# The end of a two-layer DiT kernel: gate row multiplied on GpSimd, one joining pass on VectorE, last rows stored in halves

## What is computed

```
def rms_norm(x, gain):
    xf = x.astype(jnp.float32)
    y = xf * lax.rsqrt(jnp.mean(xf * xf, axis=-1, keepdims=True) + NORM_EPS)
    return (y * gain.astype(jnp.float32)).astype(x.dtype)
...
        x = x + gt_f * rms_norm(expert_choice_ffn(h, w_router[l], w_gate[l], w_up[l], w_down[l]), g_post_f)
...
    return x
```

## Time and profile before

| | |
|---|---|
| median of 3 runs | 1984.68 us |
| the profiled execution's own time | 1987.76 us |
| its span | 1986.0 us |
| TensorE busy | 1852.5 us (93%) |
| VectorE busy | 518.4 us (26%) |
| ScalarE busy | 457.9 us (23%) |
| GpSimd busy | 158.0 us (8%) |

### The profile page before, as it was taken

One profiled execution on the slowest core, in us unless ns is written; L12 is line 12 of the kernel. 1 busy time (PEld: TensorE's weight loads), 2 busy tenths in 40 slices (PEclk: granted clock), 3 DMA queues, 4 the chain that ended last, 5 costly groups with the idle time before them and its releaser, 6 DMA issues.

```text
span 1986.0 us, 28060 instructions
## 1 busy us (share of the span) xinstructions
PE 1852.5 (93%) x12106; PEld 878.1 (44%) x12106; DVE 518.4 (26%) x1178; ACT 457.9 (23%) x961; POOL 158.0 (8%) x225
## 2 busy tenths in 40 slices
PE   4999999999899999999999999989987998888886
PEld 2555555864333333333333555568642332233322
DVE  2020576742410000000002403467433110011113
ACT  4132123533311101110112404135331111111012
POOL 0000011110011111111111000021010000000000
PEclk8999999999899999999999999999998999999998
DMA  9311187012599999999999412130159999999996
GB/s 405 132 43 54 36 355 297 23 65 85 217 357 396 414 404 410 399 418 400 411 410 374 167 43 85 43 149 23 44 192 381 426 426 426 427 427 426 427 427 249
DMA packets 54028, 540.82 MB, mean 272 GB/s; under 512 B 6528, under 2 KB 8704, under 8 KB 22960
## 3 DMA queue, kind: packets, MB, share of 16 engines
q1 hardware_dynamic: 36704, 488.82, 59.2%
q0 software_dynamic: 17088, 50.67, 7.8%
q10 hardware_dynamic: 144, 0.01, 0.0%
HBM read 515.75 MB, written 23.72 MB: 272 GB/s over the span
## 4 chain that ended last, share of the span: by engine, by line
PE 81%; DMA 12%; DVE 5%; ACT 2%; issue 1%; SPq 0%; DVEq 0%; ACTq 0%
PE ps L2089 17%; PE ps L1691 10%; PE ps L2172 9%; PE ps L1924 7%; PE ps L1668 6%; PE ps L2097 6%; DMA ring<-in_wstream 5%; DMA work<-in_wstream 3%; DMA big<-in_wstream 3%; PE ps L1871 3%; PE ps L2179 3%; PE ps L2042 2%; PE ps L1844 1%; PE ps L1615 1%; PE ps L1660 1%; PE ps L1837 1%
## 5 line engine op out<-in xcount | busy, mean ns | idle before, releaser
L2089 PE MATMUL ps<-ring,work 128*32 128x512 f32 (+1 forms) x2560 | 342.6, 596 | 12.8 <-DMA ring<-in_wstream 10.2
L1528 DVE TENSOR_TENSOR work<-glao,ps 128x512 f32<-128x512 f32 x31 | 21.3, 687 | 772.8 <-ACT glao L940 399.5
L2089 PEld LDWEIGHTS ps<-ring,work 128*32 128x32 f32 (+1 forms) x2560 | 104.6, 116 | 242.7 <-issue 228.6
L1691 PE MATMUL ps<-hT,ring 128*128 128x512 f32 (+1 forms) x592 | 208.6, 511 | 3.5 <-issue 2.1
L2172 PE MATMUL ps<-big,work 128*32 128x512 f32 (+1 forms) x1216 | 163.5, 598 | 2.1 <-ACT work L900 2.1
L1691 PEld LDWEIGHTS ps<-hT,ring 128*128 128x128 f32 x592 | 112.9, 192 | 97.1 <-issue 87.1
L1924 PE MATMUL ps<-ring,hT 128*128 128x512 f32 x320 | 138.8, 592 | 0.0
L2097 PE MATMUL ps<-ring,work 128*32 128x512 f32 x1024 | 118.9, 594 | 0.0
L1668 PE MATMUL ps<-ring,hT 128*128 128x384 f32 (+3 forms) x384 | 110.9, 451 | 0.0
L2089 PE MATMUL ps<-big,work 128*64 128x512 f32 x384 | 86.6, 595 | 15.0 <-DMA big<-in_wstream 15.0
L1924 PEld LDWEIGHTS ps<-ring,hT 128*128 128x128 f32 x320 | 60.4, 191 | 72.2 <-issue 72.2
(11 more groups left out here) (330 smaller groups left out, 2177.3 us busy)
## 6 DMA issues: line engine op xcount, KB each, us to landing
ring<-in_wstream SPq DMA_DIRECT2D x150, 2048.0 KB, 16.8
big<-in_wstream SPq DMA_DIRECT2D x68, 2048.0 KB, 18.7
hT<-in_wstream SPq DMA_DIRECT2D x12, 1024.0 KB, 30.8
work<-in_wstream SPq DMA_DIRECT2D x12, 1024.0 KB, 33.4
x_kept<-big POOLq DMA_DIRECT2D x14, 512.0 KB, 3.5
big<-x_kept POOLq DMA_DIRECT2D x12, 512.0 KB, 5.5
work<-in_nat_bias POOLq DMA_DIRECT2D x32, 128.0 KB, 2.4
xn_lat<-big POOLq DMA_DIRECT2D x8, 512.0 KB, 3.8
```

Of the source, the lines that this page charges most:

```text
L1528: V.tensor_tensor(HIDL, SGL, bank(1), ALU.mult).then_inc(sem("hid"), 1)
L1691: last = T.matmul(bank(n % 4, tn), uw[:, j * D + kc * P:j * D + kc * P + P], hTv[:, kc, t0:t0 + tn], start=kc == 0, stop=kc == KC - 1)
L2089: last = T.matmul(bank(m)[r:r + block, :], XST[:, kc, e, b:b + block], gate_up[j][kk][:, m * D + h * 512:m * D + (h + 1) * 512], start=kc ...
```

## The change

In the second layer, GpSimd now multiplies `ACC` by the gate row (without the reciprocal) into one of two buffers `GAINED`, behind its loads of `X`. It waits for the tile's `acc`, and for the third and fourth tile also until the join of the tile two back has read the buffer. VectorE no longer scales: it takes the reciprocal, waits for `gained`, and computes `GAINED * rs + X` in one pass. It no longer waits for that pass's completion. The last tile is joined in two halves of 512 columns, each followed by its own store on SyncE.

```
+        GAINED = [GAIN_X, w(tokens_at + KC * 3 * CW, D)]
...
             for t in range(NLT):
                 sp.wait_ge(sem("x_ready"), t + 1 + (DEPTH - 1) * NLT)
-                sp.dma_start(out[t * P:(t + 1) * P, :], X[:, t, :]).then_inc(sem("stored"), 16)
-            sp.wait_ge(sem("stored"), 16 * NLT)
+                if t + 1 < NLT:
+                    sp.dma_start(out[t * P:(t + 1) * P, :], X[:, t, :]).then_inc(sem("stored"), 16)
+                else:
+                    for h in range(2):
+                        c = slice(h * D // 2, (h + 1) * D // 2)
+                        sp.wait_ge(sem("x_ready"), t + 1 + h + (DEPTH - 1) * NLT)
+                        sp.dma_start(out[t * P:(t + 1) * P, c], X[:, t, c]).then_inc(sem("stored"), 16)
+            sp.wait_ge(sem("stored"), 16 * (NLT + 1))
...
                     x_again()
+                    for i, t in enumerate(tiles(l)):
+                        if i >= 2:
+                            pool.wait_ge(sem("x_ready"), i - 1 + l * NLT)
+                        pool.wait_ge(sem("acc"), LAST_ACC + i + 1)
+                        pool.tensor_tensor(GAINED[i % 2], ACC[:, t, :], GROW_F[0], ALU.mult).then_inc(sem("gained"), 1)
...
                     link(V.reciprocal(rs[:, t:t + 1], ss[:, t:t + 1]))
-                    link(V.scalar_tensor_tensor(GAIN_X, ACC[:, t, :], rs[:, t:t + 1], GROW_F[0], ALU.mult, ALU.mult))
                     dve.wait_ge(sem(f"x_rows{t}"), X_AGAIN[l])
-                    V.tensor_tensor(X[:, t, :], X[:, t, :], GAIN_X, ALU.add).then_inc(sem("x_ready"), 1)
-                    dve.wait_ge(sem("x_ready"), t + 1 + l * NLT)
+                    dve.wait_ge(sem("gained"), i + 1)
+                    for a in range(0, D, D if i + 1 < len(ts) else D // 2):
+                        c = slice(a, a + (D if i + 1 < len(ts) else D // 2))
+                        V.scalar_tensor_tensor(X[:, t, c], GAINED[i % 2][:, c], rs[:, t:t + 1], X[:, t, c], ALU.mult, ALU.add).then_inc(sem("x_ready"), 1)
                     if i + 2 < len(ts):
                         last_add(i + 2)
```

More of the change, by code:

```diff
@@ L245, in bass_hybrid_dit @@
         SQUARES, GAIN_X = w(tokens_at, D), w(tokens_at + D, D)
+        GAINED = [GAIN_X, w(tokens_at + KC * 3 * CW, D)]
+        assert KC * 3 * CW >= 2 * D and tokens_at + KC * 3 * CW + D <= outputs_at
         GROW_F = [w(picked_at + D, D), w(picked_at, D)]
```

## The result

The changed kernel takes 1989.01 us (median of 12 runs, 1986.78 to 1990.0), the one before 1984.94 us (12 runs). The ratio is 1.0018, 95% interval 1.0010 to 1.0026: slower by some 3.6 us (2.0 to 5.2). The forecast was 1986.6 us in a range up to 1988.2.

The account below looks back on a forecast made before the run. VectorE's own work and the last store were taken to set the end. With joins held, VectorE ends 2.5 us later, half stores save 0.65: +1.9 us, 1986.6 us, range 1980.2 to 1988.2.

Parts of the forecast that it names:

- Held joins: At the program's end, GpSimd's multiplications hold VectorE's joins, which have two SBUF inputs: +1.9 us, 1986.6 us; chance 0.58.
- the order: Where third multiplication and second join become ready 0.02 us apart, GpSimd gets the port first; chance 0.34.
- the nearest row to the join: L1228, without PSUM operands, took 2.29 and 2.90 us beside GpSimd multiplications instead of 0.17; so joins are held.
- The rival in which additions are held: VectorE's last additions are held by GpSimd too, so nothing overlaps from 1968.1 on: 1988.0 us; chance 0.08.
- free overlap: VectorE's joins and GpSimd's multiplications run side by side without holding: 1980.4 us, bounds 1979.5 to 1981.6; chance 0.22.
- slow sharing: Joins and GpSimd multiplications share and both take longer, without outright holding: around 1983.5 us; chance 0.12.
- The size of the hold: VectorE's work at the program's end finishes 2.5 us later than 1982.9, with held joins at 1.28 us.
- the nearest row was exact: Each GpSimd multiplication of 128x1024 with both inputs full takes 2.35 us, bounds 1.89 and 2.75.
- The rival with VectorE first: The second join wins the port before the third multiplication: +0.7 us, 1985.4 us; chance 0.24.
- The half stores: Storing the last tile in halves ends the span 0.65 us earlier, bounds 0 and 0.7.
- GpSimd's drain: Not in the prediction, which had nothing queued behind GpSimd's multiplications and the span ending with the last store.

Follow-up runs that it names:

- the best version with GpSimd: Changed kernel with joins reading X from PSUM (copied by ScalarE) and the last tile's gate multiplication on VectorE: 1982.14 us, ratio 0.9982 to the kernel before.

## Why the prediction was wrong

**Held joins: right, with luck in the order.** The joins are held at every place that the forecast named. At the first, the second multiplication was already running. At the other two I had GpSimd ready 0.02 us ahead and gave it the port for that. In the records VectorE starts first, by 0.03 and 0.04 us, and the multiplications still keep their 2.35 us while the join is held; the same happens once where the last tile's multiplication is VectorE's (1973.75 and 1973.79). So the order was forecast rightly, but not for a reason that the records bear out: that part was luck. No run has the join clearly ahead of a multiplication, so what happens then is not shown.

The experiment with X in PSUM and the one with memsets show together that, for the joining pass, the hold takes a second tensor in SBUF on VectorE and a GpSimd instruction that reads SBUF. That is what the Trainium skill's page "SBUF — State Buffer", section "Who interferes with whom", states, including that a VectorE instruction with at most one SBUF input is free of it outside what the page calls the 2-port perf modes. The trace agrees in all four combinations that were run: the join with two SBUF tensors beside a multiplication held (3.25 and 3.47 us), the join with one (1.28) and the additions with one (1.21 to 1.22) not, and the scaling pass beside a memset not (1.29). Its other statement, that whoever issues first keeps the port, can't be read off the recorded starts above, which have it the other way round by 0.03 us. And L1228 was held with a single tensor in SBUF and constants for scalars, so one input alone doesn't make every form free. The prediction passed over this difference when it took L1228 as the nearest row to the join.

The rival in which additions are held falls (1.21 to 1.22 us each), and so do free overlap and slow sharing for the kernel as it was changed. (The free overlap's upper bound of 1981.6 has three multiplications in series, not the two that its text says.)

**The size of the hold: 0.6 us too much.** VectorE's end came 1.9 us later, not 2.5. The term that was mis-sized is the held join, which I let run its full 1.28 us behind the multiplication. It ended 1.08 to 1.09 us behind it, three times, which makes 0.6. Multiplications took 2.34 to 2.36 us each; the nearest row was exact.

**The rival with VectorE first: its price was right.** I gave it an end 1.1 us earlier than the forecast's. With a wait that forces this order it measured 1.1 (16.89 against 17.99).

**The half stores: -0.65 expected, and nothing gained.** Alone they are worth 0.4 us. In the changed kernel the third tile's store was issued 0.9 and 1.5 us before the two halves of the fourth's, and the DMA engines moved all of it without a pause. DMA in 40 slices of 0.125 us over 1981 to 1986:

```profile
GB/s 0 0 0 0 0 0 0 0 0 0 459 393 426 459 328 459 328 459 360 459 213 410 328 492 295 410 361 410 377 377 410 181 0 0 0 0 0 0 0 0
```

The halves queued behind it, and the stores were done 0.2 us earlier relative to VectorE's end than before (1985.4 and 1982.93, against 1985.6 and 1982.92). Nobody profits from that, for the next reason.

**GpSimd's drain: missing, and the step that failed.** The prediction said that on GpSimd "nothing is queued behind the multiplications", and that the span ends a store's time after the last join. The program's own end stands behind them. Its drain took 6.9 us after the last multiplication and so came out 1.8 us after the stores: +1.5 us in the interval behind VectorE, where the forecast had -0.65. These 2.1 us, less the 0.6 above, are the 1.5 us by which the tail was worse than forecast (+3.4 against +1.9). The row that showed it was in the trace of the kernel before, as 11.87 us on a queue that was idle, and I had read GpSimd's idle time there as free. It ended 11.2 us behind the issue of the last load (1960.75 to 1971.97). Had I taken that as the upper bound behind the fourth multiplication's end at 1982.7, the span would have ended by 1993.9. The forecast's own end, 1985.5 and a store of 2.4, is 1987.9. The missing term would have been 0 to 6 us, and the range would have reached well over 1988.2.

With the two terms corrected the prediction's own sum gives the measured tail: 2.5 - 0.6 for VectorE and +1.5 for the end, 3.4 us. The medians differ by 4.1 and the ratio gives 3.6, which this meets within its interval.

What stays open is what the drain does in these 7 us. It is the same behind a memset of one column (6.9), four memsets (7.0) and multiplications (6.9). Where the four loads of X were the last that GpSimd issued, it ended 10.6 to 11.7 us behind the last issue, and those loads took 5.7 to 6.8 us to land. No run shows what shortens it.

## What to carry to other kernels

Before giving an idle engine the last work of a program, look at what closes its queue. Here GpSimd's drain ended 7 us after its last computing instruction, so GpSimd has to be done that long before the last store lands.

The joining pass on VectorE overlapped with GpSimd's multiplications only when one of its two tensors was in PSUM; an idle ScalarE put it there and the hold was gone. Other forms can differ: L1228 was held with a single SBUF tensor.

Forming the sums in TensorE's accumulation gave the shortest tail (13.7 us against 15.9 for the best version with GpSimd), but 2.5 us of identity matmuls ahead of it took that advantage back: over the whole program both gain the same 3.6 us.

## What the runs showed of the hardware

- GpSimd's closing drain ended 6.9 to 7.1 us behind its last computing instruction in seven kernels, for multiplications, a large memset and a memset of one column alike; ScalarE's lasted 0.23 us.
- A held VectorE pass of 1.28 us ended only 1.07 to 1.09 us after the multiplication that held it, in all seven cases of three kernels. What saves the 0.2 us is not shown.
- Several microseconds of variation between runs lie ahead of this tail. One piece is TensorE's clock. In the last down projections the granted clock was 0.81 in the profiled runs of both kernels, a mean between the two levels of 1.2 and 2.4 GHz, after a pause of 1.42 us and one of 0.69 us; in the version with three multiplications and X in PSUM it was 1.00 after the same pauses:

```profile
1954.70:1963.40 8.70, 8.70 (x32) 2.51 (x32) 0.00 (x0) 0.00 (x0) 2.18 (x4) 0.81 0.53 192
```

```profile
1949.30:1956.40 7.10, 6.29 (x31) 2.31 (x33) 0.07 (x1) 0.60 (x1) 1.78 (x4) 1.00 0.36 137
```

(The columns are the stretch, its length, the busy time of TensorE's matmuls, its weight loads, VectorE, ScalarE and GpSimd, the granted clock, the DMA share and GB/s.) The 32 matmuls took 8.7 us in the first; in the second they ran from 1950.77 to 1957.9, 7.1 us. VectorE's wait for the first contribution was 13.6 us in the profiles of both kernels under study and 11.9 in that of the second row. These 1.7 us have nothing to do with the change and are as large as half of its cost. That is why all profiles are compared from the common zero here.
